# Folding half of a modulation third on GpSimd, rating the key there, and loading the last third earlier

## The chip, the cores and the metric

One core of a Trainium2 chip runs the whole program. The metric is the time of one execution in microseconds (us) on the device; lower is better. The engines are TensorE (PE; PEld is its weight load), VectorE (DVE), ScalarE (ACT), GpSimd (POOL) and the queue SP, which issues nearly all transfers.

## The reference

Two transformer blocks run one after the other on 256 tokens of 1024 channels. The part that matters here is the start of the first block:

```
mod = c_act @ ada_w[i] + ada_b[i]                 # 1024 x 6144 weights
sh1, sc1, gt1, sh2, sc2, gt2 = split(mod, 6)
h = x * (1.0 + sc1) + sh1
p = h @ w_in[i]                                   # input projection
mla_o  = mla_group(p[..., :MLA_IN], ...)          # attention, 8 heads
rwkv_o = rwkv7_group(p[..., MLA_IN:], ...)        # recurrence, 8 heads
  # inside: a = sigmoid(...); kk = normed key; the recurrence takes kk and kk * a
x = layer_norm(ALPHA * x + (1 + gt1) * (concat(mla_o, rwkv_o) @ w_o[i]))
h = x * (1 + sc2) + sh2; then 32 experts of 1024 x 2048 and 1024 x 1024 weights
```

The first third of `mod` (sh1, sc1) is needed before the projection. The middle third (gt1, sh2) and the last third (sc2, gt2) are needed only after the recurrence. The second block (two layers of feed-forward and mixing) follows the experts.

## The kernel before

The program is a row of stages. Each has one instruction list per engine, written by hand; between stages all engines meet at a barrier. Inside a stage an engine runs its list in order, and semaphores tie the engines together. Four stages matter:

- the **projection** (Stage with exit stack `c1`): PE multiplies 18 tiles of the input weights, three products each (L767), since every tile is split in a high part (ACT, `tile_high`, L447) and a low part (DVE, `tile_low`, L451, `w_low`). The attention runs in between, two heads (a pair) at a time: PE scores (L813), DVE masks them, takes the peak (L665) and writes `shift` (L667), ACT takes exponentials (L541), DVE divides them (`divide`, L671 reciprocal and L675, four instructions), PE turns the result (`turn`, L825) and multiplies by the values. Pair p is scored behind tile 6, 8, 10 or 12 and turned behind tile 8, 10, 12 or 14;
- the **preparation** (`c4`): decays, keys and factors of the recurrence on DVE and ACT, and transposes on PE (L967) that ACT copies out (L1017);
- the **recurrence** (`c5`): chains of small 64x64 products;
- the **experts**, whose weights stream in through rings.

Before the experts `ring` has 12 slots of 128x2048 f32 (1 MB). The modulation weights come as thirds of 8 units, 1 MB each (`ada0`, `ada1`, `ada2`): unit n of `ada1` goes to slot (n+4)%8, and unit n of `ada2` to the same slot behind it. `load_ada` (L304, over `load_unit`, L289) makes SP wait on the count `used` until the slot is free. Slots 4 to 7 are free early; slots 0 to 3 hold input weights and come free tile by tile. SP issues the eight `ada1` loads at the end of its list in the projection, and the eight `ada2` loads in the preparation, behind `wo_first`.

`sum_ada` (L312) multiplies a unit by the activated conditioning vector `c_wide` (32 equal columns), four matmuls of 512 columns, and adds in `bank[3]`. PE sums `ada1` two units at a time: at the end of the projection (0, 1), and in the preparation behind `norm_spread` (2, 3), behind the transposes of v (4, 5), and behind the two transposes of `alpha_rho` and of `beta` (6 and 7). ACT copies the sums out behind its sixth transpose (L1020).

DVE's list in the preparation is: a scan, `kk` (L1033), k times `factor` (L1038), `rk` (L1040), `alpha_rho` (L1043), `kk` times `iclr` (L1045), `beta` (L1047), k times `e2` (L1048), the second half of `alpha_rho` (L1049), and `bonus` (L1053). GpSimd has nothing to do but to clear semaphores there, and nothing at all in the projection.

Of the kernel before, what the change touches and what calls it, by code (L numbers as in the profile page):

```python
# [7 lines left out]
ALU = mybir.AluOpType  # L8
# [7 lines left out]
P = 128  # L16
# [37 lines left out]
LAYER_UNITS = 2 * FFN_UNITS + MIX_UNITS + WOUT_UNITS  # L54
ADA_THIRD = ADA_UNITS // 3
ORDER = ([("ada0", n, n) for n in range(ADA_THIRD)] + [("in", n, (8 + n) % RING) for n in range(IN_UNITS)]
         + [("ada1", n, (n + 4) % 8) for n in range(ADA_THIRD)] + [("ada2", n, (n + 4) % 8) for n in range(ADA_THIRD)]
# [175 lines left out]
def build(nc, A, out, stop=None):  # L233

    with ExitStack() as ctx:
# [63 lines left out]
        def keep_busy(b, n):  # L299

            for _ in range(n):
                nc.tensor.matmul(b[:, T:T + P], ident, base[:, 0:P], start=True, stop=True, skip_group_check=True)

        def load_ada(sp, third, n):  # L304
            load_unit(sp, f"ada{third}", n, A["ada_w"][0][P * n:P * n + P, SLOT * third:SLOT * third + SLOT])

# [78 lines left out]
        with ExitStack() as c1, Stage(nc, pool, 1) as S:  # L385
# [69 lines left out]
            def _(sp):  # L455
# [20 lines left out]
                sp.dma_start(g2[:, :], A["rwkv_g2"][0]).then_inc(recurrence_in, 16)  # L476
                for n in range(ADA_THIRD):
                    load_ada(sp, 1, n)

            @S.block.scalar  # L480
# [252 lines left out]
            def _(pe):  # L733
# [149 lines left out]
                pe.sem_inc(used, 1)  # L883
                sum_ada(pe, 1, bank[3], range(0, 2))
        if stop == "mla":
# [23 lines left out]
        def wo_rows(n):  # L909
            return A["w_o"][0][T * n:T * n + T, :].rearrange("(c p) n -> p c n", p=P)  # L910
# [11 lines left out]
        with ExitStack() as c4, Stage(nc, pool, 0, S) as S:  # L922
            @S.block.gpsimd
            def _(gps):
                S.clear_former(gps)
# [4 lines left out]
            key_norm, spread, kk = ring_scratch[6][:, 0:T], ring_scratch[6][:, T:T + RW], ring_scratch[7]  # L930
            decays = ring[:, SCRATCH + 2, 0:NCH * HP * (CH + 1)].rearrange("p (h c t) -> p h c t", h=HP, c=NCH)
            factor, rk = flat(beta[:, :, :]), hT[:, 4:8, :]
# [3 lines left out]
            no_start = alpha_rho[:, 0:2, :, :].rearrange("p h x t -> p (h x t)")  # L936

            @S.block.sync
            def _(sp):
                sp.dma_start(rc[:, :], A["const_rwkv"]).then_inc(consts_loaded, 16)  # L940
                sp.dma_start(block_masks[:, :, :], A["const_blocks"]).then_inc(blocks_loaded, 16)
                sp.dma_start(wo_first[:, :, :], wo_rows(0)).then_inc(wo_first_loaded, 16)
                for n in range(ADA_THIRD):
                    load_ada(sp, 2, n)

            @S.block.tensor
            def _(pe):
# [9 lines left out]
                ins.then_inc(sem("norm_spread"), 1)  # L957
                sum_ada(pe, 1, bank[3], range(2, 4))
                pe.wait_ge(sem("acts_done"), 1)
# [11 lines left out]
                for n in range(2):  # L971
                    turn(n, lambda m: v[:, m, :])
                sum_ada(pe, 1, bank[3], range(4, 6))
                pe.wait_ge(sem("kk_ready"), 1)
# [4 lines left out]
                for which, src in enumerate((lambda m: alpha_rho[:, m, 0, :], lambda m: beta[:, m, :], lambda m: kappa[:, m, :])):  # L979
                    pe.wait_ge(sem("factors"), which + 1)  # L980
                    for a in range(TT):
                        n = 2 + 2 * which + a
                        if n >= 3:
                            pe.wait_ge(sem("nat_taken"), n - 2)
                        turn(n, src)
                    if which < 2:
                        sum_ada(pe, 1, bank[3], range(6 + which, 7 + which))

            @S.block.scalar
            def _(act):  # L990
# [23 lines left out]
                for n in range(8):  # L1014
                    which = (3, 0, 1, 2)[n // 2]
                    act.wait_ge(sem("nat_ready"), n + 1)
                    st.tell(nc.scalar.activation(nat[:, which, n % 2, :], bank[TURN_BANKS[n % 3]][:, :], ACT.Copy), "nat_taken")  # L1017
                    if n == 5:
                        act.wait_ge(used, UNIT[("ada1", ADA_THIRD - 1)] + 1)
                        nc.scalar.activation(mod_rows_1[:, :], bank[3][:, :], ACT.Copy)  # L1020

            @S.block.vector
            def _(dve):
# [15 lines left out]
                for m in range(HP):  # L1039
# [2452 lines left out]
```

## Time and profile before

| what | value |
|---|---|
| time, median of 3 runs | 2209.36 us (2208.65 to 2209.75) |
| the profiled execution's own time, and its span | 2208.19 us, 2206.4 us |
| PE, DVE, ACT, POOL busy | 95%, 54%, 35%, 1% of the span |
| projection, from its first tile to the barrier | about 34 to 117 us |
| preparation, recurrence | 117.4 to 136.5 us, 136.6 to about 205 us |
| transfers during the experts (300 to 1150 us) | 430 GB/s, busy all the time |

The busy shares are means over stages with different limits, so the argument goes stage by stage. In a timeline a row gives the start, the length, the engine, the line, the operation, `out<-in` with shapes, the count, and in brackets the idle time of the engine before it with what ended it. The busy lengths of a merged row are sums.

### The profile page before, as it was taken

Reading aid. Unit: us, or ns where it says so; the run is one execution under the profiler, and the core shown is the slowest. Engines: PE = TensorE matmul, PEld = TensorE weight load, DVE = VectorE, ACT = ScalarE, POOL = GpSimd, SP = SyncE. Lnnn points to the kernel's source line nnn. Section 1 sums busy time; section 2 is a strip of 40 time slices with the busy share of each in tenths; the row PEclk is TensorE's granted clock in tenths of the full one; section 3 lists DMA queues with packets and bytes.
Section 4 is the critical chain, followed back from the end, with each engine's and each line's share of the span. In section 5 each row is a group of like instructions: output and inputs, shape, how many; then the busy total and the mean of one; then the engine's idle time right before and its main releaser. Section 6 shows DMA issues by size and latency. Waiting matters only on the chain. (4 is left out here: it accounts for less than half of the span.)

```text
span 2206.4 us, 34205 instructions
## 1 busy us (share of the span) xinstructions
PE 2104.7 (95%) x14211; PEld 1458.3 (66%) x14211; DVE 1184.3 (54%) x1851; ACT 767.0 (35%) x1012; POOL 16.9 (1%) x18
## 2 busy tenths in 40 slices
PE   6989999999999999999999999999999999999999
PEld 5867644333334433334437889988888888988888
DVE  5765423222222222222327876788766874788874
ACT  3643311101111111011105544556544553656543
POOL 0000000000000000000000000000000000000000
PEclk9999999999999999999999999999999999999999
DMA  9355799999999999999995654544655655444652
GB/s 373 139 213 212 298 430 428 430 430 429 430 430 431 429 429 430 430 430 430 430 422 182 210 191 153 173 134 154 201 196 177 189 191 191 153 134 135 209 191 77
DMA packets 200265, 625.87 MB, mean 284 GB/s; under 512 B 13201, under 2 KB 150353, under 8 KB 164305
## 3 DMA queue, kind: packets, MB, share of 16 engines
q1 hardware_dynamic: 197536, 622.41, 72.8%
q10 hardware_dynamic: 2608, 1.72, 0.3%
q8 instruction: 92, 1.51, 0.3%
q14 instruction: 29, 0.23, 0.0%
HBM read 623.05 MB, written 1.05 MB: 283 GB/s over the span
## 5 line engine op out<-in xcount | busy, mean ns | idle before, releaser
L2256 DVE TENSOR_TENSOR w_low<-ring,w_high 128x2048 fp32r<-128x2048 f32 x168 | 386.7, 2306 | 164.8 <-ACT w_high L2251 164.8
L2251 ACT ACTIVATE w_high<-ring 128x2048 fp32r<-128x2048 f32 x168 | 320.3, 1910 | 174.2 <-PE bank L2605 140.8
L2600 PE MATMUL bank<-h_both,w_high 128*128 128x512 f32 x1344 | 322.5, 392 | 0.0
L1962 PE MATMUL bank<-ring,ut 128*64 128x512 f32 x1024 | 245.2, 629 | 37.1 <-DMA ring<-in_exp_w_dram 37.1
L2600 PEld LDWEIGHTS bank<-h_both,w_high 128*128 128x128 f32 x1344 | 246.6, 188 | 48.9
L2051 ACT ACTIVATE sg<-glu 128x512 f32<-128x512 f32 x32 | 20.2, 630 | 566.9 <-DVE glu L2124 566.9
L1929 PE MATMUL bank<-ring_odd,xt 128*64 128x512 f32 x960 | 211.4, 598 | 2.3 <-DVE lin L2127 2.3
L1929 PE MATMUL bank<-ring,xt 128*64 128x512 f32 x960 | 209.3, 594 | 0.0
L1962 PEld LDWEIGHTS bank<-ring,ut 128*64 128x64 f32 x1024 | 72.2, 143 | 194.3 <-issue 124.7
L2140 DVE SCALAR_TENSOR_TENSOR xT<-bank,mod,xT 128x256 f32<-128x256 f32 x128 | 54.2, 478 | 223.7 <-PE bank L1973 223.7
L2605 PEld LDWEIGHTS bank<-h_both,w_low 128*128 128x128 f32 x1344 | 167.4, 188 | 7.0
L2605 PE MATMUL bank<-h_both,w_low 128*128 128x256 f32 x1344 | 168.9, 278 | 0.0
L1929 PEld LDWEIGHTS bank<-ring_odd,xt 128*64 128x64 f32 x960 | 67.9, 138 | 137.4 <-issue 137.4
L2600 PE MATMUL bank<-units,w_high 128*128 128x512 f32 x640 | 155.3, 392 | 1.3 <-PEq L229 1.3
L1929 PEld LDWEIGHTS bank<-ring,xt 128*64 128x64 f32 x960 | 67.6, 137 | 133.9 <-issue 133.6
L2123 DVE TENSOR_SCALAR lin<-bank 128x256 f32<-128x256 f32 x64 | 26.7, 418 | 232.4 <-PE bank L1929 232.4
L2600 PEld LDWEIGHTS bank<-units,w_high 128*128 128x128 f32 x640 | 116.4, 188 | 23.8 <-issue 1.5
L2062 ACT ACTIVATE y_high<-bank,slot_gate 64x512 fp32r<-64x512 f32 x64 | 43.7, 682 | 219.9 <-PE bank L1962 219.1
L1602 DVE TENSOR_SCALAR choose<-base 128x64 fp32r<-128x64 f32 x68 | 14.1, 251 | 173.2 <-PE bank L1962 173.2
L2864 PE MATMUL bank<-h_both,w_high 128*128 128x256 f32 x640 | 85.4, 282 | 0.4 <-DVE h_both L2322 0.4
L2605 PEld LDWEIGHTS bank<-units,w_low 128*128 128x128 f32 x640 | 81.4, 188 | 4.4
L2605 PE MATMUL bank<-units,w_low 128*128 128x256 f32 x640 | 82.4, 278 | 0.0
(570 smaller groups left out, 2758.2 us busy)
## 6 DMA issues: line engine op xcount, KB each, us to landing
ring<-in_exp_w_dram SPq DMA_DIRECT2D x64, 2048.0 KB, 27.4
ring_odd<-in_exp_w_dram SPq DMA_DIRECT2D x64, 2048.0 KB, 27.5
ring<-in_exp_w_dram SPq DMA_DIRECT2D x128, 1024.0 KB, 25.6
ring<-in_ffn_w_gate_dram SPq DMA_DIRECT2D x44, 1024.0 KB, 5.2
ring<-in_ffn_w_up_dram SPq DMA_DIRECT2D x44, 1024.0 KB, 5.2
ring<-in_ffn_w_down_dram SPq DMA_DIRECT2D x44, 1024.0 KB, 4.8
ring<-in_w_in_dram SPq DMA_DIRECT2D x36, 1024.0 KB, 5.2
ring<-in_ada_w_dram SPq DMA_DIRECT2D x24, 1024.0 KB, 10.3
```

The costliest lines, as they stand in the source:

```text
L1602: ins = nc.vector.tensor_scalar(choose[:, side, at:at + 64], const("half_of")[:, 64 * half:64 * half + 64], const("expert_of")[:, bass.ds( ...
L1929: ins = nc.tensor.matmul(bank[b][at:at + SLOTS, :], xt[:, c, SLOTS * side:SLOTS * side + SLOTS], (ring, ring_odd)[side][:, c, 512 * q:512 ...
L1962: ins = nc.tensor.matmul(bank[first + dh][at:at + 64, :], ut[:, r % 4, rows:rows + 64], w[:, x, 512 * dh:512 * dh + 512], start=False, sto ...
L2051: nc.scalar.activation(sg[:, :], glu[:, :], ACT.Sigmoid, scale=SW_ALPHA).then_inc(sem("sg_ready"), 1)
L2062: nc.scalar.activation(y_high[at:at + 64, 512 * dh:512 * dh + 512], bank[first + dh][at:at + 64, :], ACT.Copy, scale=slot_gate[at:at + 64, ...
L2123: nc.vector.tensor_scalar(lin[:, 256 * b:256 * b + 256], pairs[:, :, 1], LIMIT, -LIMIT, ALU.min, ALU.max)
L2140: ins = nc.vector.scalar_tensor_tensor(xT[:, m, :], bank[b][:, T * j:T * j + T], mod[:, 40 + m:41 + m], xT[:, m, :], ALU.mult, ALU.add)
L2251: nc.scalar.activation(w_bufs[0][u % BUFS], ring2[:, u % RING2, :], ACT.Copy).then_inc(high2, 1)
L2256: nc.vector.tensor_tensor(w_bufs[1][u % BUFS], ring2[:, u % RING2, :], w_bufs[0][u % BUFS].bitcast(F32), ALU.subtract).then_inc(low2, 1)
L2600: return nc.tensor.matmul(b[:, :], w_parts[0][:, at:at + P], moving.rearrange("p a t -> p (a t)"), start=start, stop=False, skip_group_che ...
L2605: return nc.tensor.matmul(b[:, 0:T], w_parts[1][:, at:at + P], moving[:, 0, :], start=False, stop=stop, skip_group_check=True)
L2864: ins = nc.tensor.matmul(b[:, T * x:T * x + T], w[:, at:at + P], h[:, c, :], **flags)
```

## The change

- During the projection GpSimd multiplies each of the units 0 to 3 of `ada1` by its column of the conditioning vector and adds units 1 to 3 into unit 0, in place: four multiplications and three additions on 128x2048 f32. PE sums the folded unit with four matmuls by ones (`sum_folded`), which counts four units as used.
- The slots of the folded units 1 to 3 take the `ada2` units 1 to 3 as soon as each is folded; the other `ada2` loads stay in the preparation, and `wo_first` goes behind them.
- PE sums units 4 and 5 at the end of the projection, 6 and 7 earlier in the preparation, and nothing between the last transposes. ACT copies the sums out behind the second transpose.
- GpSimd computes `kk` times `iclr` in the preparation into `kk_rated`; DVE waits for it instead, and for `rk_ready`.

```diff
+        def sum_folded(pe, b):
+            for j in range(4):
+                ins = nc.tensor.matmul(b[32 * j:32 * j + 32, :], ones[:, 0:32], ring[:, unit_slot("ada1", 0), 512 * j:512 * j + 512],
+                                       start=True, stop=False, skip_group_check=True)
+            ins.then_inc(used, FOLDED)
...
+            @S.block.gpsimd
+            def _(gps):
...
+                st.step(nc.gpsimd.tensor_scalar(total, total, c_wide[:, 0, 0:1], None, ALU.mult))
+                for n in range(1, FOLDED):
...
+                    unit_ready(gps, "ada1", n)
+                    st.step(nc.gpsimd.tensor_scalar(unit, unit, c_wide[:, n, 0:1], None, ALU.mult))
+                    st.step(nc.gpsimd.tensor_tensor(total, total, unit, ALU.add), "folded")
...
-                sum_ada(pe, 1, bank[3], range(0, 2))
+                pe.wait_ge(sem("folded"), FOLDED - 1)
+                sum_folded(pe, bank[3])
+                sum_ada(pe, 1, bank[3], range(4, 6))
...
+                gps.wait_ge(sem("kk_ready"), 1)
+                gps.wait_ge(sem("acts_done"), 2)
+                gps.wait_ge(sem("csum_ready"), 1)
+                nc.gpsimd.tensor_tensor(kk_rated, kk, iclr, ALU.mult).then_inc(sem("kk_rated"), 1)
...
-                st.step(nc.vector.tensor_tensor(kk, kk, iclr, ALU.mult))
+                dve.wait_ge(sem("kk_rated"), 1)
                 dve.wait_ge(sem("exps"), 2)
-                st.tell(nc.vector.tensor_tensor(flat(beta[:, :, :]), kk, e2, ALU.mult), "factors")
+                dve.wait_ge(sem("rk_ready"), 1)
+                st.tell(nc.vector.tensor_tensor(flat(beta[:, :, :]), kk_rated, e2, ALU.mult), "factors")
```

GpSimd before, from the program's start to the recurrence (the branches lead from stage to stage, the ISA row clears semaphores):

```order
L3478 MEMSET const-uint8-127 128x1
L923 UNCONDITIONAL_BRANCH
L222 ISA
L225 UNCONDITIONAL_BRANCH
L1063 UNCONDITIONAL_BRANCH
```

GpSimd after, from the projection to the end of the preparation (`ring` holds the units and, in the last row, `kk`, `iclr` and `kk_rated`):

```order
L503 TENSOR_SCALAR ring<-ring,c_wide 128x2048
L507 TENSOR_SCALAR ring<-ring,c_wide 128x2048
L508 TENSOR_TENSOR ring<-ring 128x2048
L507 TENSOR_SCALAR ring<-ring,c_wide 128x2048
L508 TENSOR_TENSOR ring<-ring 128x2048
L507 TENSOR_SCALAR ring<-ring,c_wide 128x2048
L508 TENSOR_TENSOR ring<-ring 128x2048
L226 UNCONDITIONAL_BRANCH
L967 UNCONDITIONAL_BRANCH
L223 ISA
L973 TENSOR_TENSOR ring<-ring 128x1024
```

Seven long instructions stand beside the projection where there were none, and one in the preparation.

SP before, from its last small loads in the projection to the recurrence:

```order
L476 DMA w_kv<-in_rwkv_g2_dram 128x512
L289 DMA ring<-in_ada_w_dram 128x2048 x8
L225 UNCONDITIONAL_BRANCH
L938 UNCONDITIONAL_BRANCH
L940 DMA rwkv_const<-in_const_rwkv_dram 128x192
L941 DMA block_masks<-in_const_blocks_dram 128x768
L942 DMA wo_first<-in_w_o_dram 128x2x1024
L289 DMA ring<-in_ada_w_dram 128x2048 x8
```

SP after (L493 is an `ada2` unit that goes out behind a fold, L290 any other unit):

```order
L290 DMA ring<-in_ada_w_dram 128x2048 x4
L493 DMA ring<-in_ada_w_dram 128x2048
L290 DMA ring<-in_ada_w_dram 128x2048
L493 DMA ring<-in_ada_w_dram 128x2048
L290 DMA ring<-in_ada_w_dram 128x2048
L493 DMA ring<-in_ada_w_dram 128x2048
L290 DMA ring<-in_ada_w_dram 128x2048 x2
L226 UNCONDITIONAL_BRANCH
L975 UNCONDITIONAL_BRANCH
L977 DMA rwkv_const<-in_const_rwkv_dram 128x192
L290 DMA ring<-in_ada_w_dram 128x2048 x5
L982 DMA wo_first<-in_w_o_dram 128x2x1024
```

Three of the eight `ada2` loads moved into the projection, and `wo_first` to the end.

PE before, in the second half of the preparation (L312 sums units, L967 transposes, L977 is the bonus product):

```order
L312 MATMUL bank<-ring,c_wide 32x512 x8
L961 MATMUL bank<-ps,w_kv 128x256 x4
L967 MATMUL bank<-base,ps 128x128 x8
L312 MATMUL bank<-ring,c_wide 32x512 x8
L977 MATMUL bank<-hT,base 128x512 x2
L967 MATMUL bank<-base,alpha_rho 128x128 x8
L312 MATMUL bank<-ring,c_wide 32x512 x4
L967 MATMUL bank<-base,beta 128x128 x8
L312 MATMUL bank<-ring,c_wide 32x512 x4
L967 MATMUL bank<-base,ps 128x128 x8
```

PE after, at the same place (L323 sums, L1005 transposes, L1015 is the bonus product):

```order
L323 MATMUL bank<-ring,c_wide 32x512 x4
L999 MATMUL bank<-ps,w_kv 128x256 x4
L1005 MATMUL bank<-base,ps 128x128 x8
L323 MATMUL bank<-ring,c_wide 32x512 x4
L1015 MATMUL bank<-hT,base 128x512 x2
L1005 MATMUL bank<-base,alpha_rho 128x128 x8
L1005 MATMUL bank<-base,beta 128x128 x8
L1005 MATMUL bank<-base,ps 128x128 x8
```

Four of the six units' sums are gone from here, two of them from between the last transposes.

## Rows read from the trace of the kernel before

**Rows 1.** PE's waits, whole span: for whom, total us, times, longest us.

```profile
PE bank L1962 <- DMA ring<-in_exp_w_dram: 37.1, 18, 4.0
...
PE bank L1160 <- issue: 2.3, 3, 1.2
```

**Rows 2.** Busy time by stretch: PE, PEld, DVE, ACT, POOL; then PEclk, DMA share, GB/s.

```profile
300.00:1150.00 850.00, 806.87 (x3921) 332.21 (x3921) 240.84 (x604) 91.08 (x151) 0.00 (x0) 0.98 1.01 430
```

**Rows 3.** Timeline of the projection, DVE and then PE, around the first attention pair.

```profile
71.69 0.16 DVE L667 TENSOR_TENSOR shift<-peak,q_scale 128x4 f32<-128x4 f32 x1
...
72.96 1.22 DVE L451 TENSOR_TENSOR w_low<-ring,w_high 128x1024 fp32r<-128x1024 f32 x1
...
74.65 0.42 DVE L650 TENSOR_TENSOR diff<-raw,bank 128x256 f32<-128x256 f32 x1 [0.47 <-ACT raw L521]
...
75.92 1.01 DVE L675 TENSOR_SCALAR ring<-ring,den 128x128 f32<-128x128 f32 x4
...
76.98 0.87 PE L825 MATMUL bank<-base,ring 128*128 128x128 f32 x6
```

**Rows 4.** SP's issue of the first two ada1 units, and the first unit's landing.

```profile
54.30 0.90 SPq L289 DMA_DIRECT2D ring<-in_ada_w_dram  x2
...
ring<-in_ada_w_dram SPq DMA_DIRECT2D x1, 1024.0 KB, 8.5
```

**Rows 5.** Timeline of the second block: GpSimd and VectorE side by side and alone.

```profile
1370.36 0.87 DVE L2322 SCALAR_TENSOR_TENSOR h_both<-xT,params,h_both 128x256 fp32r<-128x256 f32 x2
...
1371.18 2.74 POOL L2833 TENSOR_TENSOR hT<-hT 128x512 f32<-128x512 f32 x2 [1370.72 <-ACT hT L2318]
1371.53 2.67 DVE L2322 SCALAR_TENSOR_TENSOR h_both<-xT,params,h_both 128x256 fp32r<-128x256 f32 x2 [0.30 <-ACT h_both L2317]
...
1373.99 1.35 POOL L2836 TENSOR_TENSOR hT<-hT 128x512 f32<-128x512 f32 x1
1374.12 3.37 DVE L2256 TENSOR_TENSOR w_low<-ring,w_high 128x2048 fp32r<-128x2048 f32 x1
...
1379.76 2.28 DVE L2256 TENSOR_TENSOR w_low<-ring,w_high 128x2048 fp32r<-128x2048 f32 x1
...
1455.16 3.23 POOL L2845 COPY hT<-hT 64x512 f32<-64x512 f32 x2 [69.66 <-DVE hT L3262]
1455.33 2.59 DVE L2256 TENSOR_TENSOR w_low<-ring,w_high 128x2048 fp32r<-128x2048 f32 x1
```

**Rows 6.** Timeline of the projection's end, PE and DVE.

```profile
114.28 1.92 PE L312 MATMUL bank<-ring,c_wide 128*32 128x512 f32 x16
...
116.67 0.48 DVE L651 SCALAR_TENSOR_TENSOR ps<-diff,params,bank 128x256 f32<-128x256 f32 x1
```

**Rows 7.** Timeline of the preparation, DVE.

```profile
124.29 1.22 DVE L1038 TENSOR_TENSOR ps<-ps,beta 128x1024 f32<-128x1024 f32 x1
...
125.55 1.68 DVE L1040 SCALAR_TENSOR_TENSOR hT<-ps,params 128x256 f32<-128x256 f32 x4
...
128.27 1.22 DVE L1045 TENSOR_TENSOR ring<-ring 128x1024 f32<-128x1024 f32 x1
...
133.02 1.28 DVE L1053 TENSOR_TENSOR bonus<-bank,ps 128x512 f32<-128x512 f32 x2
```

**Rows 8.** Timeline of the preparation, PE and ACT.

```profile
128.77 1.98 PE L977 MATMUL bank<-hT,base 128*128 128x512 f32 x4
...
130.59 1.04 PE L967 MATMUL bank<-base,alpha_rho 128*128 128x128 f32 x8
...
134.58 1.09 PE L967 MATMUL bank<-base,ps 128*128 128x128 f32 x8
...
135.27 1.08 ACT L1017 ACTIVATE nat<-bank 128x512 f32<-128x512 f32 x2
```

**Rows 9.** Timeline of the recurrence's start, PE.

```profile
143.12 1.04 PE L1169 MATMUL bank<-beta,alpha_rho 64*64 64x64 f32 x56 [3.44 <-issue]
```

**Rows 10.** Busy time by stretch, as in the second group, inside that wait.

```profile
140.00:142.00 2.00, 0.00 (x0) 0.00 (x0) 0.40 (x2) 0.00 (x0) 0.00 (x0) 1.00 1.02 418
```

More of the change, by code:

```diff
@@ L55 @@
 ADA_THIRD = ADA_UNITS // 3
+FOLDED = 4
 ORDER = ([("ada0", n, n) for n in range(ADA_THIRD)] + [("in", n, (8 + n) % RING) for n in range(IN_UNITS)]
@@ L476, in _ @@
                 sp.dma_start(g2[:, :], A["rwkv_g2"][0]).then_inc(recurrence_in, 16)
-                for n in range(ADA_THIRD):
+                for n in range(FOLDED):
                     load_ada(sp, 1, n)
+                for n in range(1, FOLDED):
+                    slot = unit_slot("ada2", n)
+                    sp.wait_ge(sem("folded"), n)
+                    sp.dma_start(ring[:, slot, :], ada_rows(2, n)).then_inc(loaded[slot], 16)
+                    load_ada(sp, 1, FOLDED - 1 + n)
+                load_ada(sp, 1, ADA_THIRD - 1)
+            @S.block.gpsimd
+            def _(gps):
+                st = Steps(gps, sem, "gps_step")
+                total = ring[:, unit_slot("ada1", 0), :]
+                gps.wait_ge(sem("c_wide_ready"), 1)
+                unit_ready(gps, "ada1", 0)
+                st.step(nc.gpsimd.tensor_scalar(total, total, c_wide[:, 0, 0:1], None, ALU.mult))
+                for n in range(1, FOLDED):
+                    unit = ring[:, unit_slot("ada1", n), :]
+                    unit_ready(gps, "ada1", n)
+                    st.step(nc.gpsimd.tensor_scalar(unit, unit, c_wide[:, n, 0:1], None, ALU.mult))
+                    st.step(nc.gpsimd.tensor_tensor(total, total, unit, ALU.add), "folded")
             @S.block.scalar
@@ L930, in build @@
             key_norm, spread, kk = ring_scratch[6][:, 0:T], ring_scratch[6][:, T:T + RW], ring_scratch[7]
+            kk_rated = sig
             decays = ring[:, SCRATCH + 2, 0:NCH * HP * (CH + 1)].rearrange("p (h c t) -> p h c t", h=HP, c=NCH)
@@ L936, in build, with _ @@
             no_start = alpha_rho[:, 0:2, :, :].rearrange("p h x t -> p (h x t)")
+            @S.block.gpsimd
+            def _(gps):
+                S.clear_former(gps)
+                gps.wait_ge(sem("kk_ready"), 1)
+                gps.wait_ge(sem("acts_done"), 2)
+                gps.wait_ge(sem("csum_ready"), 1)
+                nc.gpsimd.tensor_tensor(kk_rated, kk, iclr, ALU.mult).then_inc(sem("kk_rated"), 1)
             @S.block.sync
@@ L941, in _ @@
                 sp.dma_start(block_masks[:, :, :], A["const_blocks"]).then_inc(blocks_loaded, 16)
+                load_ada(sp, 2, 0)
+                for n in range(FOLDED, ADA_THIRD):
+                    load_ada(sp, 2, n)
                 sp.dma_start(wo_first[:, :, :], wo_rows(0)).then_inc(wo_first_loaded, 16)
-                for n in range(ADA_THIRD):
-                    load_ada(sp, 2, n)
             @S.block.tensor
@@ L957, in _ @@
                 ins.then_inc(sem("norm_spread"), 1)
-                sum_ada(pe, 1, bank[3], range(2, 4))
+                sum_ada(pe, 1, bank[3], range(6, 7))
                 pe.wait_ge(sem("acts_done"), 1)
@@ L972, in _ @@
                     turn(n, lambda m: v[:, m, :])
-                sum_ada(pe, 1, bank[3], range(4, 6))
+                sum_ada(pe, 1, bank[3], range(7, 8))
                 pe.wait_ge(sem("kk_ready"), 1)
@@ L985, in _ @@
                         turn(n, src)
-                    if which < 2:
-                        sum_ada(pe, 1, bank[3], range(6 + which, 7 + which))
             @S.block.scalar
```

9 lines of the change are left out of this document (4 added, 5 removed).

## The prediction

> **What bounds the kernel now.** I read the busy table by stretch first, then the waits, then the timelines of the stages that the edit touches. Through the experts (300 to 1150 us) the transfer engines are busy all the time at 430 GB/s, and PE's greatest wait in the whole program is 37.1 us for expert weights [rows 1, 2]. That stretch is bound by transfers whose start hangs on the stages ahead of it, and behind it nothing is touched. So a microsecond won or lost between 55 and 200 us moves the end by a microsecond, and the question is only what the projection, the preparation and the start of the recurrence gain or lose.
>
> In the projection PE runs without a gap, but DVE is hardly ahead of it. The first attention pair shows it: DVE divides from 75.92 for 1.01 us, to 76.93, and PE turns these probabilities at 76.98 [rows 3]. Whatever holds DVE ahead of that division holds PE, 0.05 us later. The other three pairs repeat this.
>
> In the preparation one chain runs through DVE, PE's last transposes and ACT's last copies, which end at 136.35 (135.27 + 1.08) [rows 8]. At the start of the recurrence PE stands still for 3.44 us, waiting for nothing the trace names ("issue"), in the middle of one run of small products [rows 9]. During it the transfer engines are full, at 418 GB/s [rows 10]. Another line of this stage has three waits of the kind, of 1.2 us at most [rows 1]. I take the 3.44 us for the fetch of PE's own instructions, queued behind the last `ada2` units.
>
> **The fold in the projection: a loss.** GpSimd itself has time: PE wants the folded unit only behind the last tile, at 114.28 [rows 6]. The trouble is what it does to DVE. In the second block GpSimd adds 512 columns in 1.35 us, starting 0.13 us ahead of a `w_low` on DVE; that one takes 3.37 us where it takes 2.28 alone, 1.09 more [rows 5]. Two GpSimd adds in 2.74 us lengthen two DVE instructions from 0.87 to 2.67 us, 0.90 for each add [rows 5]. So a DVE instruction with two inputs in SBUF waits until GpSimd has nearly ended, and one gets in between two of GpSimd's. Behind two GpSimd copies of 512 columns `w_low` grows by 0.31 only, but the copies take 3.23 us: the 2.28 us of `w_low` lie between them, and a copy itself takes (3.23 - 2.28) / 2 = 0.48 us [rows 5].
>
> The Trainium skill, SBUF — State Buffer, section "SBUF: two separate sides", says that DVE and GpSimd share one read and one write port pair, held for a whole instruction, against DVE instructions with two SBUF inputs or in a two-port mode. The rows agree for two inputs; for the two-port mode (the divisions, if the page holds) no row here shows it.
>
> From these rows: an add of 2048 columns holds DVE for 4 x 0.9 to 4 x 1.09, 3.6 to 4.4 us; I take 4.0, and 4.3 for its whole turn, since the recorded 1.35 is 0.3 longer than the hold. The upper bound is 4 x 1.35 = 5.4. A multiplication reads one input, like the copy: 4 x 0.48 = 1.9 us, and at the least 4 x 0.31 = 1.2; the copies' raw mean of 1.6 us would give 6.4, which I use only for the range. The Trainium skill, GPSIMD Engine Reference, section 3.1, gives 4497 ns for an add of 2048 f32 columns; with it each add would be 0.2 us longer, and the sum about 0.4 us.
>
> Now in order of time. Unit 0 lands at 54.30 + 8.5 = 62.8 [rows 4], the others some 2.4 us apart (1 MB at 430 GB/s [rows 2]). GpSimd multiplies unit 0 (to 64.7), unit 1 (to 66.7), adds (to 71.1), multiplies unit 2 (to 73.1), adds (to 77.5). DVE wants `shift` at 71.69: both inputs are in SBUF, so it waits to about 73.0. The two evictions behind it read PSUM and run on, to 74.3. `w_low`, due at 72.96, finds the second add and waits to 77.4; it ends at 78.6 instead of 74.18, 4.4 us late [rows 3]. Between the next instruction's start (74.65, which ACT had held by 0.47) and the divisions' (75.92) lie 1.27 us [rows 3]: 79.9. Whether a division, with one input, waits for GpSimd no row shows; I count that it does, and the third multiplication (78.6 to 80.4) then costs 0.5. The divisions end at 81.4 instead of 76.93: PE's first turn is 4.5 us late. The third add then runs behind the next `w_low`, from 82.6 to 86.7, and holds the second pair's `shift`, due some 3 us behind that `w_low` (an estimate, by the first pair's steps), at 85.5, by 1.2 us, which PE meets at the second turn. Then GpSimd is done, and PE, never ahead of its work, catches nothing up: **+5.7 us**. With holds of 3.6 and 1.2 it is +3.5, with 5.4 +8.5; below nothing it can't go, since nothing is taken from DVE or PE here. If DVE's idle time covered all, it would be 0. PE's three sums at the end in place of two add 0.9 us to 116.2, 117.1, beside DVE's own end at 116.67 + 0.48 = 117.15 [rows 6]: nothing; without that cover, 0.9.
>
> **The preparation: a gain.** GpSimd's `kk_rated` becomes ready to start when DVE goes on to k times `factor` (124.29 to 125.51) [rows 7], which gets in first. DVE then waits for its own result, GpSimd gets the port, and 1024 columns hold it 2 x 1.0 = 2.0 us: `rk` starts at 127.5 and ends at 129.2 instead of 127.23. The multiplication that left DVE was 1.22 us [rows 7], so DVE is 0.8 us later and ends at 133.02 + 1.28 + 0.8 = 135.1 [rows 7]. PE's bonus product waits for `rk` and starts at 129.3 (before: 128.77); the first transpose follows 1.82 us later as before (130.59) [rows 8], 131.1; the next two, with no sums between, each 1.0 us behind. The last starts at 133.1 instead of 134.58, 1.5 us earlier, and ACT ends at about 134.9. The stage ends with DVE at 135.1 instead of 136.35: **-1.2 us**. If the engines did not collide, DVE would end at 133.1, and ACT at 132.9 since bonus starts at 127.3: -3.3. If `kk_rated` held DVE for its full 2.7 us, -0.5. Moving ACT's copy of the sums from the sixth to the second transpose costs nothing: ACT then waits for PE.
>
> SP's waits on `folded` stand ahead of the loads of `ada1` units 4 to 7. Those can't go before PE releases the input slots, the first as it begins tile 12, three tiles and a pair's attention behind the first turn, which is later than the third fold's end at about 87. So nothing behind them in the queue is delayed, and `wo_first` at the queue's end is not used before the recurrence is over.
>
> **The start of the recurrence: a gain.** Three of the `ada2` loads are gone from the preparation, 3 MB, some 7 us at 430 GB/s, and the seventh unit's slot comes free earlier against the stage's end. So the instruction fetch finds the transfer engines free, and the wait falls from 3.44 to the other waits' 1.2 us: **-2.2 us**. Bounds: -3.4 if it vanishes, 0 if the transfers have no part in it.
>
> **Sum.** 5.7 - 1.2 - 2.2 = +2.3 us. On the profiled execution's 2208.19 us that is 2210.5; this execution lies 1.2 us below the median of 2209.36, so in terms of the median 2211.7. 0.2% is 4.4 us, about what a measurement of this kernel can tell from no change. With its own bounds this case reaches from 2208.3 (3.5 - 1.2 - 3.4 = -1.1) to 2213.2 (adds of 4.4, kk_rated in full: 6.5 - 0.5 - 2.2 = +3.8).
>
> **Rivals.**
> *No collision in the projection.* If DVE's idle time before 70 us takes most of the fold, or its instructions get between GpSimd's more often than the rows say, the projection keeps its length and the preparation gains in full: -3.3 - 2.2 = -5.5, **2203.9**. For it: most DVE instructions there read PSUM. Against it: the 1.09 and 0.90 us of [rows 5], and the 0.05 us of [rows 3].
> *A dearer fold.* An add that holds DVE for its whole recorded length (5.4 us), or one that gets in between the four divisions of a pair, so that PE's turn waits a whole add of 4.0 where I count 1.2: either way +8.5 instead of +5.7. With `kk_rated` at its full length: 8.5 - 0.5 - 2.2 = +5.8, **2215.2**. It decides from a loss of 7.8 us in the projection on (4.4 + 3.4). For it: four short divisions in a row leave GpSimd four places to get in, if they need the port. Against it: only one add is left by then.
> *The wait at 139 us isn't the transfers'.* If it is the place in the code, the 3.44 us stay: +4.5, **2213.9**. For it: it is PE's sequencer that stands still, in every execution at one place. Against it: the 1.2 us of the other waits of its kind [rows 1], and the full transfer engines [rows 10].
>
> **How the numbers follow.** The forecast has a chance of 0.50, no collision 0.17, the dearer fold 0.23, the wait that stays 0.10. Faster by over 0.2%: three quarters of the no-collision case and a trace of the first, 0.14. Slower by over 0.2%: nearly all of the dearer fold (0.21), half of the wait that stays (0.05) and the forecast's upper end (0.05), 0.31. Within: 0.55. Eight in ten lie between 2205 (most of the no-collision case outside) and 2217.5 (the dearer fold inside, but for multiplications at the copies' raw 1.6 us per 512 columns, which would hit more pairs).
>
> **What would show it.** Right: the first `w_low` and the first division behind GpSimd's second add some 4 us longer or later, PE's first turn waiting for DVE 4 to 5 us, the second about 1; no PE wait at the last two turns; `rk` about 2 us longer; PE's "issue" wait in the first products near 1 us. Wrong: DVE instructions of their old length beside GpSimd's (then 2204), PE waiting at three or four turns or for `folded` (then 2217 and more), or the 3.4 us still there with the transfer engines idle.

## The result: slower, 2223.6 us, and where the time went

| | before | after |
|---|---|---|
| median of four runs | 2209.56 us | 2223.58 us |
| profiled execution, its span | 2208.19, 2206.4 us | 2222.1, 2220.3 us |
| projection's end (the preparation's first product) | 117.47 us | 136.00 us |
| preparation (to the recurrence's first product) | 19.19 us | 17.87 us |
| from there to SP's first `wo` load | 49.07 us | 46.69 us |

The ratio is 1.0064, with a 95% interval from 1.0051 to 1.0076. The predicted time was 2211.7 us, its range 2205.0 to 2217.5: the result lies outside. Two of the three terms came out in size (-1.32 us in the preparation for a predicted -1.2, -2.38 behind it for -2.2). The projection became 18.53 us longer where +5.7 was predicted.

First GpSimd's timeline after the change (start us, length us, engine, line, operation):

```profile
63.00 6.43 POOL L503 TENSOR_SCALAR ring<-ring,c_wide 128x2048 f32<-128x2048 f32 x1 [62.55 <-DMA ring<-in_ada_w_dram]
69.52 5.44 POOL L507 TENSOR_SCALAR ring<-ring,c_wide 128x2048 f32<-128x2048 f32 x1
75.05 5.38 POOL L508 TENSOR_TENSOR ring<-ring 128x2048 f32<-128x2048 f32 x1
80.53 5.55 POOL L507 TENSOR_SCALAR ring<-ring,c_wide 128x2048 f32<-128x2048 f32 x1
86.16 4.52 POOL L508 TENSOR_TENSOR ring<-ring 128x2048 f32<-128x2048 f32 x1
90.78 6.30 POOL L507 TENSOR_SCALAR ring<-ring,c_wide 128x2048 f32<-128x2048 f32 x1
97.17 4.51 POOL L508 TENSOR_TENSOR ring<-ring 128x2048 f32<-128x2048 f32 x1
```

The unit lands when it should (63.0, predicted 62.8). A multiplication takes 5.4 to 6.4 us, not 1.9, and GpSimd goes from one instruction to the next without a gap, to 101.68 us. Beside it DVE's rows that answer to [rows 3], from its timeline, and the first two of the four divisions apart, from shorter stretches of it:

```profile
74.77 1.22 DVE L462 TENSOR_TENSOR w_low<-ring,w_high 128x1024 fp32r<-128x1024 f32 x1
77.72 8.57 DVE L705 TENSOR_SCALAR ring<-ring,den 128x128 f32<-128x128 f32 x4
86.22 5.56 DVE L462 TENSOR_TENSOR w_low<-ring,w_high 128x1024 fp32r<-128x1024 f32 x1
98.15 4.34 DVE L705 TENSOR_SCALAR ring<-ring,den 128x128 f32<-128x128 f32 x4
...
77.72 2.79 DVE L705 TENSOR_SCALAR ring<-ring,den 128x128 f32<-128x128 f32 x1
...
80.70 5.46 DVE L705 TENSOR_SCALAR ring<-ring,den 128x128 f32<-128x128 f32 x1
```

The four divisions, 1.01 us in [rows 3], take 8.57 us. The first stands to 80.51, behind the addition that ends at 80.43; the multiplication starts at 80.53, between two divisions, and another division stands from 80.70 to 86.16, behind it (80.53 + 5.55 = 86.08). The second pair's stand to 101.77, behind the last addition (97.17 + 4.51 = 101.68). TensorE's turns wait for that:

```profile
86.35 1.54 PE L855 MATMUL bank<-base,ring 128*128 128x128 f32 x6 [7.47 <-DVE ring L705]
102.55 1.45 PE L855 MATMUL bank<-base,ring 128*128 128x128 f32 x6 [4.43 <-DVE ring L705]
112.97 0.82 PE L855 MATMUL bank<-base,ring 128*128 128x128 f32 x6
...
136.00 1.31 PE L988 MATMUL bank<-ps,w_kv 64*128 64x256 f32 x5 [0.42 <-PEq L226]
```

In the kernel before, the first turn starts at 76.98 [rows 3]; the second, the third and the preparation's first product are:

```profile
85.74 0.82 PE L825 MATMUL bank<-base,ring 128*128 128x128 f32 x6
...
94.44 0.82 PE L825 MATMUL bank<-base,ring 128*128 128x128 f32 x6
...
117.47 1.32 PE L950 MATMUL bank<-ps,w_kv 64*128 64x256 f32 x5 [1.27 <-PEq L225]
```

So after is 9.37, 16.81 and 18.53 us late, and from the third turn on nothing is added. What lies between two turns beside the waits is the clock. Its granted value by stretch (us, then busy us and instructions of PE, PEld, DVE, ACT, POOL; PEclk, DMA share, GB/s):

```profile
76.00:79.00 3.00, 2.88 (x25) 2.67 (x23) 2.36 (x4) 2.48 (x7) 3.00 (x1) 1.00 0.00 0
85.00:88.00 3.00, 1.65 (x8) 1.65 (x9) 3.00 (x3) 0.07 (x1) 2.92 (x2) 0.50 0.00 0
88.00:91.00 3.00, 3.00 (x12) 2.64 (x12) 3.00 (x1) 1.68 (x2) 2.90 (x2) 0.50 0.00 0
103.00:106.00 3.00, 3.00 (x14) 2.73 (x12) 1.44 (x3) 1.75 (x2) 0.00 (x0) 0.50 0.03 5
```

Behind each of the two waits TensorE runs at 0.50, the level of 1.2 GHz, where it ran at 2.4 GHz ahead of it. The stretch from the first turn's start to the next tile's first row behind that pair's attention is 8.63 us (86.35 to 94.98) in place of 5.79 (76.98 to 82.77), behind the second 7.44 in place of 5.73: 2.84 and 1.71 us more. With the waits that is 7.47 + 2.84 + 4.43 + 1.71 = 16.45 us, or 16.7 by the starts of the rows, whose ends overlap a little. The other 1.8 us were there before the fold began: 0.2 ahead of 50 us, and 1.6 at 50.7 us, where the granted clock was 0.75 from 50 to 53 us and a product of 1.99 us took 3.06 (the "low-clock row" below). It isn't the change's: the run with the key alone has such a row, the run with the multiplications alone hasn't.

Behind the projection the change gave what was expected of it. From DVE's and PE's timelines:

```profile
144.07 3.67 DVE L1076 SCALAR_TENSOR_TENSOR hT<-ps,params 128x256 f32<-128x256 f32 x4
...
157.46 0.69 PE L1206 MATMUL bank<-beta,alpha_rho 64*64 64x64 f32 x32 [0.21 <-issue]
```

`rk` is 2.0 us longer than in [rows 7], as counted, and the wait of 3.44 us [rows 9] is 0.21.

### The profile page after: what moved, and what is told of

It is laid out like the page before. It is cut to its first block and busy times, and to the rows that moved or that the text cites. A ratio compares the mean times of both kernels' runs of the same rounds, so it can differ in the third digit from the quotient of the medians.

```text
span 2220.3 us, 34170 instructions
## 1 busy us (share of the span) xinstructions
PE 2109.3 (95%) x14187; PEld 1461.6 (66%) x14187; DVE 1200.8 (54%) x1850; ACT 766.6 (35%) x1012; POOL 58.4 (3%) x26
## 5 line engine op out<-in xcount | busy, mean ns | idle before, releaser
L1999 PE MATMUL bank<-ring,ut 128*64 128x512 f32 x1024 | 249.1, 639 | 35.4 <-DMA ring<-in_exp_w_dram 35.2
```

The source lines that it names most:

```text
L1999: ins = nc.tensor.matmul(bank[first + dh][at:at + 64, :], ut[:, r % 4, rows:rows + 64], w[:, x, 512 * dh:512 * dh + 512], start=False, sto ...
```

## Experiments: is it GpSimd, and by what

The theory after this trace: the fold costs by holding DVE, above all the divisions; loads, sums and order bring the gain. The rival: the loads and the later sums cost.

**The fold without its arithmetic.**

```diff
-                st.step(nc.gpsimd.tensor_scalar(total, total, c_wide[:, 0, 0:1], None, ALU.mult))
+                st.step(nc.gpsimd.memset(gps_mark[:, :], 0.0))
...
-                    st.step(nc.gpsimd.tensor_scalar(unit, unit, c_wide[:, n, 0:1], None, ALU.mult))
-                    st.step(nc.gpsimd.tensor_tensor(total, total, unit, ALU.add), "folded")
+                    st.step(nc.gpsimd.memset(gps_mark[:, :], 0.0), "folded")
```

> The changed kernel without the fold's arithmetic: GpSimd waits for the units and signals as before, but each of its seven long operations is a fill of one column, so the units are not folded and the modulation sums are of other data. Loads, sums, key and order of work stay. If GpSimd's operations cause the loss (by holding the divisions, and through the stalls TensorE's clock), the divisions are back at 1.01 us, both of TensorE's waits for them (7.47 and 4.43 us) are gone, and what is left of the change is the two gains after the projection (1.29 and 2.41 us): about 2205.8 us, 0.998 of the kernel before. The rival, that the moved loads and the fewer sums cause the loss, gives the time of the changed kernel, about 2223 us. Gains in the projection of over 2 us against before would be unexpected.

2204.06 us, ratio 0.998 (0.997 to 0.999). The first pair's divisions in its trace:

```profile
77.76 1.01 DVE L705 TENSOR_SCALAR ring<-ring,den 128x128 f32<-128x128 f32 x4
```

No turn waits. The projection is 1.84 us longer than before, 0.2 of it ahead of 50 us and the rest by the low-clock row at 50.76 us (3.16 us); the preparation takes 17.87. So the loss is GpSimd's arithmetic: 16.7 us of projection between this trace and the changed kernel's (136.00 - 119.31; both have the low-clock row). The rest of the change is a gain of 5.4 us against before, 1.7 more than expected. These two make +11.3 us, not the +14.0 of the medians: another 1.6 us stand in the recurrence, where this trace comes to SP's first `wo` load in 45.10 us and the changed kernel's in 46.69. What makes these isn't shown; in the ten traces in which the wait of 3.44 us is gone and nothing is loaded later, this stretch runs from 45.10 to 47.93.

**Multiplications alone.** The three additions are left out.

```diff
-                    st.step(nc.gpsimd.tensor_scalar(unit, unit, c_wide[:, n, 0:1], None, ALU.mult))
-                    st.step(nc.gpsimd.tensor_tensor(total, total, unit, ALU.add), "folded")
+                    st.step(nc.gpsimd.tensor_scalar(unit, unit, c_wide[:, n, 0:1], None, ALU.mult), "folded")
```

> The changed kernel with the fold's three additions left out (the four multiplications stay; the sums are of other data). GpSimd is busy from 63 to about 86.5 us only. If the multiplications alone hold the divisions, the first pair's wait of 4 to 9 us for TensorE stays and the second pair's goes, and w_low is back at 1.22 us everywhere: 2210 to 2215 us. The rival, that the additions alone do the holding, gives 2204 to 2206 us.

2216.65 us, ratio 1.0033 (1.0022 to 1.0045), 1.7 above the theory's end. Two of GpSimd's multiplications, then DVE's and PE's:

```profile
73.47 6.01 POOL L507 TENSOR_SCALAR ring<-ring,c_wide 128x2048 f32<-128x2048 f32 x1
...
79.57 5.44 POOL L507 TENSOR_SCALAR ring<-ring,c_wide 128x2048 f32<-128x2048 f32 x1
...
75.91 9.31 DVE L704 TENSOR_SCALAR ring<-ring,den 128x128 f32<-128x128 f32 x4
85.14 1.21 DVE L462 TENSOR_TENSOR w_low<-ring,w_high 128x1024 fp32r<-128x1024 f32 x1
...
85.28 1.54 PE L854 MATMUL bank<-base,ring 128*128 128x128 f32 x6 [8.21 <-DVE ring L704]
```

The divisions stand through the rest of one multiplication and the whole of the next. So the multiplications hold them without any addition. The second pair's turn waits for nothing. Of the 1.7 us, 1.4 can be seen in the preparation, which took 19.23 us in this trace at a granted clock of 0.73 (140 to 143 us) and 0.54 (142 to 145).

**The division with two inputs.**

```diff
-                            ins = nc.vector.tensor_scalar(part, part, den[:, a, x:x + 1], None, ALU.mult)
+                            ins = nc.vector.tensor_tensor(part, part, den[:, a, x:x + 1].to_broadcast([P, KEYS[a]]), ALU.mult)
```

> The changed kernel with the division by the sums written with two inputs on VectorE (the row times its reciprocal spread along it) in place of one input and a scalar; same numbers, same order, the fold stays whole. My theory: GpSimd's multiplications hold only VectorE's one-input instructions, its additions hold both kinds (in the changed kernel w_low took 1.22 us beside a multiplication and 5.56 us behind an addition). Then the first turn's divisions wait for one addition only and TensorE goes on about 4.5 us earlier, and the second's, now some 5 us earlier, fall beside a multiplication and aren't held: the time falls by 6 to 10 us, to 2213 to 2218 us. The rival, that GpSimd holds VectorE whatever the form, leaves it at 2223 us.

2218.93 us, ratio 1.0044 (1.0026 to 1.0061): above the expected range, and this reading of the trace fell. GpSimd's rows, then DVE's (the second from a short stretch):

```profile
80.56 5.81 POOL L507 TENSOR_SCALAR ring<-ring,c_wide 128x2048 f32<-128x2048 f32 x1
91.12 5.45 POOL L507 TENSOR_SCALAR ring<-ring,c_wide 128x2048 f32<-128x2048 f32 x1
...
81.06 3.85 DVE L705 TENSOR_TENSOR ring<-ring,den 128x256 f32<-128x256 f32 x1
...
91.23 4.68 DVE L462 TENSOR_TENSOR w_low<-ring,w_high 128x1024 fp32r<-128x1024 f32 x1
```

A multiplication does hold two-input work, but not to its end: the division started at 81.06 is done at 84.91, 1.46 us ahead of the multiplication's end, and `w_low`, which takes 1.22 alone, is held 3.46 us and done at 95.91, 0.66 ahead of it. The `w_low` of 1.22 us in the changed kernel, from which I had read that multiplications don't hold, came 5.25 us into one. The two-input division gains little in the trace (the projection ends at 135.83), since the second pair's divisions still meet the last addition; the median is 4.7 us lower than the changed kernel's, but the runs go from 2215.9 to 2226.2.

**The division on ScalarE.**

```diff
-                            ins = nc.vector.tensor_scalar(part, part, den[:, a, x:x + 1], None, ALU.mult)
+                                ins = nc.scalar.activation(part, part, ACT.Copy, scale=den[:, a, x:x + 1])
```

> The changed kernel with the division made by ScalarE (four copies with a scale of each pair of heads), VectorE keeping the reciprocal; the fold stays whole. If the held divisions are the loss, both of TensorE's waits (7.47 and 4.43 us) go but for what the held w_low (5.56 us behind an addition) and ScalarE's own 1.5 us for each pair cost: 2208 to 2213 us. The rival, that the fold costs the projection in other ways too (the held w_low, the later sums), leaves it above 2217 us.

2215.96 us, ratio 1.0034 (1.0018 to 1.005), from 2211.3 to 2221.0 us run by run: between the two cases. The turns wait 0.39, 1.81, 2.11 and 1.47 us for ACT in place of 7.47 and 4.43 for DVE, and the projection ends at 124.35, in the trace of the fastest of the five runs and without the low-clock row. So the held divisions are the larger part of the loss (7.6 us of the median). What is left is ACT's own 1.49 us for each pair, now on the path, what that delays (`w_low` waits 2.51 us for ACT's `w_high` behind each), and the held `w_low`; how much is whose, no run separates.

**Multiplications with two tensors.**

```diff
-                    st.step(nc.gpsimd.tensor_scalar(unit, unit, c_wide[:, n, 0:1], None, ALU.mult))
+                    st.step(nc.gpsimd.tensor_tensor(unit, unit, c_wide[:, n, 0:1].to_broadcast([P, SLOT]), ALU.mult))
```

> The changed kernel with GpSimd's four multiplications written with two tensors (the factor spread along the row) in place of a tensor and a scalar. If a multiplication then takes an addition's 4.5 us in place of 5.4 to 6.3, the fold ends about 6 us earlier and the held divisions with it: 2217 to 2219 us. The rival, that a multiplication's time is not its form's, or that more of VectorE's two-input work is held, leaves it at 2223 us or above.

2220.34 us, ratio 1.0053 (1.0037 to 1.0069).

```profile
75.20 3.60 POOL L507 TENSOR_TENSOR ring<-ring,c_wide 128x2048 f32<-128x2048 f32 x1
...
88.12 4.66 POOL L508 TENSOR_TENSOR ring<-ring 128x2048 f32<-128x2048 f32 x1
...
88.44 1.54 PE L855 MATMUL bank<-base,ring 128*128 128x128 f32 x6 [9.52 <-DVE ring L705]
100.67 0.88 PE L855 MATMUL bank<-base,ring 128*128 128x128 f32 x6 [1.78 <-DVE ring L705]
```

The form sets the length: 3.6 to 4.5 us where a scalar operand takes 5.4 to 6.4. The fold ends 8.9 us earlier (92.78), the second wait shrinks to 1.78, but the first grows to 9.52, since more `w_low` are held (3.62 and 5.55 us). Both answers were half right. The projection ends 3.5 us earlier in the trace (132.48); the median is 3.2 us lower, though the intervals overlap.

**TensorE kept busy in its waits.**

```diff
+                    if p < 2:
+                        keep_busy(bank[2], (30, 17)[p])
+                    pe.wait_ge(sem("probs_scaled"), p + 1)
```

> The changed kernel, with TensorE given 30 and 17 matmuls of no use before the first and second turn, in the time in which it waits for the divisions. The divisions stay held. If the slow stretch after each stall is the clock's (granted 0.50 after the stalls; the stretches cost 2.84 and 1.71 us more than in the kernel before), the clock stays at 1.00 and the time falls by about 4.5 us to 2219 us. The rival, that these stretches are long because the work itself is late (GpSimd's add still holds w_low for 5.56 us), gives no change, 2223 us.

2223.56 us, ratio 1.0067 (1.005 to 1.0084): no change. (Each of the 30 and 17 matmuls is two rows of the trace, 60 and 34.) The clock stays at 1.00 behind the first turn and the stretch is back at 5.78 us; the second turn starts at 102.46 all the same, since GpSimd's last addition releases it. So the first 2.84 us are not on the path. With 62 useless rows in place of 34 at the second wait too:

```diff
-                        keep_busy(bank[2], (30, 17)[p])
+                        keep_busy(bank[2], (30, 31)[p])
```

> The changed kernel with TensorE kept busy through both of its waits (60 and 62 matmuls of no use in place of 60 and 34). In the run before it the granted clock stayed at 1.00 through the first wait and the 2.84 us came back there, but the second turn began at 102.46 us all the same, as its divisions wait for GpSimd's last addition; the 34 matmuls ended 3.53 us ahead of it and the clock fell. If what is left of the clock's cost is that behind the second turn, it goes: 1.7 us less than the changed kernel, 2221 to 2222.5 us, and the turn's stretch to the next tile's first row is about 5.7 us in place of 7.44. The rival, that the projection's end hangs on VectorE there as well, gives 2223.5 us.

2221.64 us, ratio 1.0057 (1.0043 to 1.007). The second turn and the end of its attention (next tile's first row):

```profile
102.43 0.87 PE L857 MATMUL bank<-base,ring 128*128 128x128 f32 x6 [0.42 <-DVE ring L705]
...
108.21 1.21 PE L797 MATMUL bank<-h_high,w_high 128*128 128x256 f32 x8
```

5.78 us in place of 7.44, and the projection ends at 134.21 in place of 136.00. The time agrees with 1.7 us, but the intervals overlap; the rows carry it.

**The key.** Back on DVE in the changed kernel:

```diff
-                nc.gpsimd.tensor_tensor(kk_rated, kk, iclr, ALU.mult).then_inc(sem("kk_rated"), 1)
...
+                st.step(nc.vector.tensor_tensor(kk, kk, iclr, ALU.mult))
```

> The changed kernel with the key rated on VectorE again as in the kernel before; the fold stays. My theory puts nearly all of the loss in the projection and a gain of under 1.3 us in the preparation, of which the shared gate of VectorE's rk (3.67 us in place of 1.68) eats a part: the time stays within 1 us of the changed kernel's, 2222.6 to 2224.5 us. The rival, that rating on GpSimd costs the preparation several us, gives 2219 or less.

And alone in the kernel before:

```diff
+                nc.gpsimd.tensor_tensor(kk_rated, kk, iclr, ALU.mult).then_inc(sem("kk_rated"), 1)
...
-                st.step(nc.vector.tensor_tensor(kk, kk, iclr, ALU.mult))
```

> The kernel before with one part of the change alone: GpSimd rates the key in the preparation; no fold, loads and sums as before. VectorE's four rk instructions then share the port with it (1.68 to about 3.7 us) and its own rating of 1.22 us goes: VectorE is 0.8 us later. My prediction took this as a part of a net gain; the run of the changed kernel with the key back on VectorE came out 2.6 us faster than the changed kernel, of which its trace shows 0.70 us in the preparation. By the first the time is 0.3 to 0.8 us over the kernel before, 2209.8 to 2210.3 us; the rival, that rating on GpSimd costs 2 us or more, gives 2211.5 us or more.

The first: 2220.94 us, ratio 1.0057 (1.004 to 1.0073). The second: a median of 2211.37, ratio 1.0003 (0.9994 to 1.0013), no difference that could be told; its runs go from 2208.4 to 2212.2 us, so the time doesn't decide between the two answers. The preparations say more: 17.14 us with the key back, 17.87 without; 19.74 with the key alone, 19.19 before. Rating on GpSimd costs 0.73 and 0.55 us. That the first gained 2.6 us in the time, over my bound, isn't clear of noise, as the intervals overlap. It has a candidate: with the key on GpSimd TensorE waits 2.25 us for `rk`, and in the trace of the run with both waits filled the product behind it took 3.15 us (1.96 in the changed kernel's trace) at a granted clock of 0.62, and the preparation 19.31. Of the eight traces with this key and these sums it came in two (the other is that with the multiplications alone), which is too few to tell how often.

**The loads.** In the kernel before, no GpSimd; the sums earlier in the preparation; two `ada2` units and `wo_first` put off:

```diff
+                sp.wait_ge(sem("a2v_ready"), 1)
+                for n in range(ADA_THIRD - 2, ADA_THIRD):
+                    load_ada(sp, 2, n)
+                sp.dma_start(wo_first[:, :, :], wo_rows(0)).then_inc(wo_first_loaded, 16)
                 sp.wait_ge(sem("n_ready"), 1)
```

> The kernel before with the two gains of the change taken without GpSimd: the modulation's middle third is summed wholly by TensorE and earlier (three units, three units, none between the last transposes), and the last two units of the last third and the first wo rows are loaded after the recurrence has begun. If the wait of 3.44 us at the recurrence's start came from the last loads, it goes, and with the shorter end of the preparation (1.2 us) the time is about 2206 us, faster than both kernels. The rival, that the loads put off are missed later (the wo units or the expert weights start 2 to 4 us later and the expert part is bound by transfers), gives 2209 to 2211 us.

2208.83 us, ratio 0.9997 (0.9987 to 1.0006): no difference. PE's timeline, and the busy time where the loads now run and behind them:

```profile
140.07 1.04 PE L1170 MATMUL bank<-beta,alpha_rho 64*64 64x64 f32 x56 [0.69 <-issue]
180.27 0.28 PE L1253 MATMUL bank<-nat,ring 64*64 64x64 f32 x4 [2.19 <-issue]
```

```profile
172.00:175.00 3.00, 3.00 (x60) 3.00 (x57) 1.84 (x3) 2.93 (x7) 0.00 (x0) 1.00 1.03 426
175.00:178.00 3.00, 2.42 (x137) 2.27 (x133) 2.78 (x8) 1.47 (x3) 0.00 (x0) 1.00 0.90 367
178.00:181.00 3.00, 0.81 (x56) 0.73 (x52) 1.89 (x6) 0.28 (x1) 0.00 (x0) 1.00 0.03 12
```

The wait at the start has shrunk from 3.44 to 0.69 us, and one of 2.19 us stands where the loads went, just behind their end. Spread over three places:

```diff
+                sp.wait_ge(sem("low_turned"), 1)
+                load_ada(sp, 2, ADA_THIRD - 2)
+                sp.wait_ge(sem("x_taken0"), 3)
+                load_ada(sp, 2, ADA_THIRD - 1)
+                sp.wait_ge(sem("x_taken0"), 4)
+                sp.dma_start(wo_first[:, :, :], wo_rows(0)).then_inc(wo_first_loaded, 16)
```

> The kernel before without GpSimd, as in the run with the last loads put off, whose wait at the recurrence's start went from 3.44 to 0.69 us while one of 2.19 us came up where the put-off loads ran (169 to 178 us); here the three loads are spread over the recurrence, one behind its products and one behind each of two levels. If TensorE's waits follow the transfers, each load can catch one of them and adds up to 1 to 2 us, or none if it falls between two: 2206 to 2209 us, and the wait of 2.19 us is back under 1. The rival, that these waits have nothing to do with the loads, leaves 2.19 us where it was and gives 2208.8 us.

2209.89 us, ratio 1.0004 (0.9994 to 1.0013), above the expected range. The busy time where the second and third loads run, then PE's timeline:

```profile
156.00:159.00 3.00, 2.53 (x119) 2.40 (x114) 2.30 (x4) 1.01 (x2) 0.00 (x0) 1.00 0.82 265
165.00:168.00 3.00, 3.00 (x145) 2.93 (x146) 1.85 (x3) 1.23 (x3) 0.00 (x0) 0.94 0.72 206
```

```profile
162.17 0.37 PE L1134 MATMUL bank<-ring 64*64 64x64 f32 x2 [2.45 <-issue]
171.56 1.07 PE L1163 MATMUL bank<-ring 64*64 64x64 f32 x23 [2.87 <-issue]
```

The 2.19 us are gone from 180 us, and 2.45 and 2.87 us stand behind the two later loads; the first (142 to 146 us) brought no wait over 0.71 until 150 us. Behind these two waits the granted clock was 0.50 (162 to 165 us) and 0.69 (171 to 174), which the expectation had left out. Over three kernels a wait of over 2 us went where the transfers went. The moved waits begin as the loads end, though, and waits of up to 1.65 us stand where nothing is loaded (the changed kernel at 199.70 us, DMA share 0.01). That it is TensorE's instructions that come late agrees with the trace (a packet of 0.02 MB on the instruction queue about every 4 us here), but no run separates it from another cause that goes with transfers.

**The fold on VectorE, in its gaps.** The gains kept, the holding gone:

```diff
+                        unit_ready(dve, "ada1", 0)
+                        st.step(nc.vector.tensor_scalar(total, total, c_wide[:, 0, 0:1], None, ALU.mult))
...
+                    st.tell(nc.vector.scalar_tensor_tensor(total, unit, c_wide[:, n, 0:1], total, ALU.mult, ALU.add), "folded")
```

> The change with the fold on VectorE in place of GpSimd, put where VectorE waits in the kernel before: one multiplication and one multiply-and-add in its idle 3.80 us ahead of the row at 68.75, one more multiply-and-add each in its idle 2.32 us ahead of 109.67 and 2.82 us ahead of 113.42; the key is rated on VectorE as before, three units of the last third are loaded as their slots come free. By my theory (the fold cost through what GpSimd holds, and the gains lie in the three units that TensorE no longer sums and in the loads that end before the recurrence) nothing is held, the projection keeps its length, the preparation is about 2 us shorter and the wait of 3.44 us at the recurrence's start is gone: 2204 to 2206 us, faster than both kernels. The rival, that about 2.2 us for each VectorE instruction overrun the gaps and hold TensorE, gives 2209 or more.

2206.15 us, ratio 0.9984 (0.9975 to 0.9993): faster than both kernels, at the expected range's upper end.

```profile
66.66 1.29 DVE L756 TENSOR_SCALAR ring<-ring,c_wide 128x2048 f32<-128x2048 f32 x1
67.98 2.35 DVE L706 SCALAR_TENSOR_TENSOR ring<-ring,c_wide 128x2048 f32<-128x2048 f32 x1
70.43 0.42 DVE L673 TENSOR_TENSOR diff<-raw,bank 128x256 f32<-128x256 f32 x1
...
140.08 0.69 PE L1207 MATMUL bank<-beta,alpha_rho 64*64 64x64 f32 x32 [0.42 <-issue]
```

The row at 70.43 stood at 68.75 before, and all of the 1.68 us between them were already there at 62.77 (61.09 before), from the low-clock row at 50.6 us: the fold delays nothing. The preparation is 17.13 us, the wait 0.42.

## Why the prediction was wrong, step by step

The price that failed came from GpSimd's two copies of [rows 5]. Shorter stretches of the same trace show them one by one:

```profile
1455.16 0.60 POOL L2845 COPY hT<-hT 64x512 f32<-64x512 f32 x1 [69.66 <-DVE hT L3262]
...
1455.83 2.56 POOL L2845 COPY hT<-hT 64x512 f32<-64x512 f32 x1
```

The first takes 0.60 us. The second ends 0.47 us behind the `w_low` beside it (1455.33 + 2.59 = 1457.92), so it did wait for that, as the prediction supposed.

1. **What bounds the kernel: right.** The loss of 18.53 us, less 3.70 gained to SP's first `wo` load, makes 14.83 there, and 13.9 at the end (about 1 us came back in the experts, whose wait for weights fell from 37.1 [rows 1] to 35.2).
2. **A multiplication at 1.9 us: the step that failed.** I priced it by GpSimd's copies of [rows 5], since both read one input; the trace before has no GpSimd multiplication. Measured are 5.4 to 6.4. Four multiplications add 23.7 us and not 7.6, so the fold ends at 101.68 in place of 86.7 and meets the second pair whole. The additions, at 4.5 to 5.4 for 4.3, were nearly right. The copies I had read rightly (0.60 us alone, four times that 2.4 us), but they were the wrong stand-in. That the raw mean times four, 6.4 us, comes near the measured length is chance, and the stated range left this very case out.
3. **A division's wait behind a multiplication at 0.5 us: failed with it.** That a one-input instruction waits was counted, but the price followed from the short multiplication (the fourth of the working, called the third there); it was 5.46 us. The Trainium skill, SBUF — State Buffer, section "SBUF: two separate sides", says that DVE in a two-port mode waits for a whole GpSimd instruction; the divisions wait so (to 86.16 for an end at 86.08), though no run shows their mode. For two inputs, where the page has the whole instruction as well, the measured hold by a multiplication was 1.9 us shorter than it. One reading of the working was wrong, too: the other three pairs don't repeat the 0.05 us of the first, their divisions end 0.54 us ahead of the turn (84.19 + 1.01 for 85.74), so a hold costs 0.5 us less there. How the bounds of +3.5 and +8.5 come about, the working doesn't show.
4. **The clock at nothing: missed.** 1.7 us behind the second turn. The first turn's 2.84 us cost nothing in the end.
5. **The rival "a dearer fold" named the mechanism**, an instruction of GpSimd between two divisions, but with an addition, at 4.0 us, and only once. The sign "PE waiting at three or four turns" didn't come: two turns, of 4 to 7 us, were enough to pass 2217.
6. **Preparation: right; recurrence: right in part by luck.** -1.32 us for -1.2, made of -2.05 by the sums (17.14 us with the key back against 19.19) and +0.7 by the key (predicted +0.8). The -2.38 for -2.2 is made of two misses: the wait fell by 3.23 us, to 0.21 and not to 1.2, and 0.85 us came up again later in the stretch. With the measured terms the sum is 16.7 - 1.3 - 2.4 = +13.0, for +14.0 between the medians (by the interval, 11.3 to 16.8). The 16.7 are 15.0 to the second turn (16.81 less the 1.8 from before the fold), set by GpSimd's end, and 1.7 behind it, set by the clock.

## What to carry to other kernels

An engine with time to spare isn't free if its instructions hold those of an engine that has none: count, for each instruction that it gets, which instructions of the other stand behind it, and price it by a row of the same form. Here GpSimd's copy (0.60 us for 512 columns) said nothing about its multiplication by a scalar (5.4 to 6.4 us for 2048). Where the trace has no such row, and two estimates lie apart by three, the dearer one belongs into the stated range. The same work in known gaps of the busy engine (8.3 us in 8.9 idle us ahead of three rows) cost nothing here.

## What was not expected of the hardware

- GpSimd's multiplication with a scalar from memory (5.4 to 6.4 us for 2048 columns) is longer than one with two tensors (3.6 to 4.5) and than an addition (4.5 to 5.4). DVE does it in 1.29 us.
- A GpSimd multiplication with a scalar holds DVE's one-input divisions to its end, two-input work only up to 3.6 to 4.4 us from its start, 1.9 us ahead of its end (`w_low` at 91.23 beside the division on two inputs; `shift`, 0.80 us for 0.16, at 94.57 in the changed kernel).
- TensorE's wait of 3.44 us at the recurrence's start fell to 0.21 to 0.91 where no transfers ran beside it, and waits of over 2 us came up behind three of the four places to which the loads were put (2.19; 2.45 and 2.87).
- In eight of the fourteen traces TensorE's clock was lower for a few us behind a wait of 1.42 us at 50.6 us, in the others not, with and without the fold; it costs 1.6 us there (7.5 us from that product's start to the next tile's, for 5.86), and its cause is open.
